# Splitting an expert table into f16 halves in earlier stages, and loading it as halves

## What is computed

```python
qh = (xb @ w_pq).reshape(t, PEER_HEADS, 2, PEER_QDIM // 2)
s = jnp.einsum('thpc,hpkc->thpk', qh, peer_keys)
s_top, i_top = lax.top_k(s, PEER_TOPK)
...                                   # 16 best of 256 pairs of each head: idx, softmax g
u = peer_u[idx]
a = jax.nn.gelu(jnp.einsum('td,ted->te', xb, u), approximate=False)
w = (g * a)
return jnp.einsum('te,ted->td', w, peer_v[idx])
```

## Time and profile before

| what | value |
|---|---|
| median of 3 runs | 4344.81 us (4338.82 to 4346.47) |
| profiled execution, its own time | 4337.67 us |
| its span | 4335.7 us |
| PE, DVE, ACT, POOL busy | 83%, 73%, 30%, 22% of the span |
| DMA | 856.46 MB, mean 198 GB/s |

### The profile page before, as it was taken

How to read it: one execution, slowest core, us unless ns; L and a number is a source line. 1 busy time by engine, 2 the same in 40 slices (tenths; PEclk the granted TensorE clock), 3 DMA queues, 4 the chain that set the end, 5 groups by cost and what they waited for, 6 DMA issues and landing times. The chain is left out here.

```text
span 4335.7 us, 59165 instructions
## 1 busy us (share of the span) xinstructions
PE 3612.2 (83%) x19538; PEld 1998.8 (46%) x19538; DVE 3183.3 (73%) x5656; ACT 1302.0 (30%) x2576; POOL 939.4 (22%) x1038
## 2 busy tenths in 40 slices
PE   6956468899689757487899999999999999999993
PEld 3535344455345423366345454544444454454442
DVE  1024431222459978899699999999899999999998
ACT  2131222211223233344233332333333333332331
POOL 0000000000000000000344444444443444444444
PEclk9966569999899878655899999999999999999996
DMA  2100020210211010266788888889888888888885
GB/s 92 63 26 1 0 84 29 99 38 0 84 61 38 22 62 0 79 194 193 293 337 328 340 330 327 331 323 341 314 329 326 326 334 324 341 325 319 334 329 184
DMA packets 238936, 856.46 MB, mean 198 GB/s; under 512 B 16080, under 2 KB 119312, under 8 KB 167440
## 3 DMA queue, kind: packets, MB, share of 16 engines
q0 software_dynamic: 73728, 536.90, 32.7%
q1 hardware_dynamic: 165136, 318.63, 21.2%
HBM read 792.55 MB, written 62.91 MB: 197 GB/s over the span
## 5 line engine op out<-in xcount | busy, mean ns | idle before, releaser
L1579 POOL COPY x_index<-expert 128x1 uint32 (+1 forms) x512 | 333.9, 652 | 2951.2 <-POOLq L1379 2068.0
L70 PE MATMUL x_ps_v<-x_v_hi,x_w_hi 128*128 128x512 f16 x1536 | 604.6, 394 | 134.4 <-DVE x_w_lo L1683 77.5
L1582 POOL DMA_INDIRECT x_rows<-in_peer_uv,x_index x512 | 581.9, 1137 | 406.9 <-POOL x_index L1579 393.1
L1653 DVE SCALAR_TENSOR_TENSOR acc<-x_rows,x_share,acc 128x1024 f32<-128x1024 f32 x512 | 654.8, 1279 | 0.0
L1737 PE MATMUL x_ps_a<-h_hi,x_u_hi 128*128 128x256 f16 (+1 forms) x2048 | 620.5, 327 | 18.4 <-ACT x_u_hi L1595 15.8
L1738 PE MATMUL x_ps_a<-h_lo,x_u_hi 128*128 128x256 f16 (+1 forms) x2048 | 620.2, 327 | 0.0
L71 PE MATMUL x_ps_v<-x_v_lo,x_w_hi 128*128 128x512 f16 x1536 | 603.8, 393 | 0.0
L72 PE MATMUL x_ps_v<-x_v_hi,x_w_lo 128*128 128x512 f16 x1536 | 602.3, 392 | 0.0
L1606 ACT ACTIVATE x_dots<-x_dots 128x1 f32<-128x1 f32 x512 | 103.9, 203 | 1328.4 <-DVE x_dots L1671 1328.4
L1671 DVE CUSTOM_DVE_ANT_0 x_rows<-h_lo,x_rows 128x1024 f32<-128x1024 f32 x256 | 312.4, 1220 | 124.5 <-DMA x_rows<-in_peer_uv,x_index 123.5
L1742 PE MATMUL x_ps_a<-h_hi,x_u_lo 128*128 128x256 f16 (+1 forms) x2048 | 374.6, 326 | 0.0
(11 more groups left out here) (286 smaller groups left out, 6398.2 us busy)
## 6 DMA issues: line engine op xcount, KB each, us to landing
x_u_st<-in_peer_u_t SPq DMA_DIRECT2D x128, 512.0 KB, 5.9
x_v_st<-in_peer_v SPq DMA_DIRECT2D x128, 512.0 KB, 5.8
gate_scratch<-g_out SPq DMA_DIRECT2D x24, 2048.0 KB, 8.7
x_gate<-gate_scratch SPq DMA_DIRECT2D x32, 1024.0 KB, 8.7
x_gate<-gate_scratch SPq DMA_DIRECT2D x32, 512.0 KB, 3.7
m_w_st<-in_w_merge SPq DMA_DIRECT2D x8, 1536.0 KB, 6.4
k_w_st<-in_w_route SPq DMA_DIRECT2D x16, 576.0 KB, 3.7
x_rows<-in_peer_uv,x_index POOLq DMA_INDIRECT x512, 6.9
```

Of the source, the lines that this page charges most:

```text
L70: pe.matmul(out, lhs_hi, rhs_hi, start=first, stop=False)
L1579: pool.tensor_copy(index[:, m % RING:m % RING + 1], R.expert[:, tile, bass.ds(hk, 1)]).then_inc(index_ok, 1)
L1582: pool.indirect_dma_start(rows[:, m % RING], None, uv_all, bass.IndirectOffsetOnAxis(ap=index[:, m % RING:m % RING + 1], axis=0)).then_inc ...
L1653: dve.scalar_tensor_tensor(R.acc[:, DT + tile], rows[:, r, D:2 * D], share[:, s:s + 1], R.acc[:, DT + tile], ALU.mult, ALU.add).then_inc(v ...
```

## The change

In project and merge a new helper, Ahead, reads all 128 tiles of table v (40 in project, 88 in merge) by DMAs that POOL issues, splits them with ACT (high half, times 4) and DVE (low half), and stores the two halves, 512 KB for a tile as before, in a scratch of device memory (v_scratch). It has two buffers: the load of tile n waits for the low half of tile n - 2, and stands behind its store. In project a split stands behind each of the ten evacuations of the values and behind each block of ten weight tiles; in merge, 4, 4 and 3 splits stand in the three blocks of a weight tile. Experts then loads the halves into one buffer for each of the four expert tiles, without splits; these loads wait for the last product of the group before. Each stage's semaphores are now cleared and given back when it ends, with one more barrier (release).

```diff
+class Ahead:
...
+    def load(self, pool, A, n, s, first=False):
+        if not first:
+            pool.wait_ge(self.v_lo_ok, n - 1)
+        pool.dma_start(self.st[:, s], A["peer_v"][n + self.first]).then_inc(self.v_in[s], 16)
+
+    def high(self, act, n, s, nth, first=False):
+        act.wait_ge(self.v_in[s], 16 * nth)
+        if not first:
+            act.wait_ge(self.v_out[s], 16 * nth - 16)
+        act.activation(self.out[:, s, 0], self.st[:, s], ACT.Copy, scale=VSCALE).then_inc(self.v_hi_ok, 1)
+
+    def low(self, dve, n, s):
+        dve.wait_ge(self.v_hi_ok, n + 1)
+        dve.scalar_tensor_tensor(self.out[:, s, 1], self.st[:, s], VSCALE, self.out[:, s, 0], ALU.mult,
+                                 ALU.subtract).then_inc(self.v_lo_ok, 1)
+
+    def store(self, pool, n, s):
+        pool.wait_ge(self.v_lo_ok, n + 1)
+        pool.dma_start(self.R.v_dram[n + self.first], self.out[:, s]).then_inc(self.v_out[s], 16)
+
+    def moves(self, pool, A, count):
+        self.load(pool, A, 0, 0, True)
+        self.load(pool, A, 1, 1, True)
+        with pool.Fori(0, count // 2 - 1) as i:
+            for s in range(2):
+                self.store(pool, 2 * i + s, s)
+                self.load(pool, A, 2 * i + (2 + s), s)
...
@@ project, ACT
                     act.activation(R.proj[:, m, t0:t0 + n_t], ps[:, slot, b, 0:n_t], ACT.Copy,
                                    scale=1 / WSCALE).then_inc(m_ev, 1)
+                    if turn is not None:
+                        ahead.high(act, TT + 6 * turn + (at + b), (at + b) % 2, 3 * turn + (TT // 2 + (at + b) // 2 + 1))
...
@@ merge
+        SHARE = (4, 4, 3)
...
@@ merge, ACT
+                    early, late = units(i, q, b)
+                    for v, slot, nth in early:
+                        ahead.high(act, v, slot, nth, isinstance(v, int) and v < 2)
                     wait_apart(act, mg_ok, n + 1)
                     act.activation(R.m_hi[:, m, t0:t0 + n_t], mg[:, s, 0:n_t], ACT.Copy).then_inc(mg_hi, 1)
+                    for v, slot, nth in late:
+                        ahead.high(act, v, slot, nth)
...
@@ Buffers
+    def release(self):
+
+        self.nc.clear_and_free_semaphores(self.stage)
+        self.stage = []
+        self.nc.all_engine_barrier()
...
@@ experts, SP
             def load_v(i, e, first=False):
-                n = E * i + e
-                if not first or e >= 2:
-                    sp.wait_ge(v_lo_ok, n - 1)
-                sp.dma_start(v_st[:, e % 2], v_all[n]).then_inc(v_in[e % 2], 16)
+                if not first:
+                    wait_apart(sp, v_mm, V_STEPS * i)
+                sp.dma_start(v[:, e], R.v_dram[E * i + e]).then_inc(v_in, 16)
...
@@ experts, ACT
-                        if b == 0:
-                            act.wait_ge(v_in[e % 2], 32 * i + 16 * (e // 2 + 1))
-                            if not first:
-                                act.wait_ge(v_mm, V_STEPS * i)
-                            act.activation(v_hi[:, e], v_st[:, e % 2], ACT.Copy, scale=VSCALE).then_inc(v_hi_ok, 1)
...
@@ experts, DVE
-                        if b == 0:
-                            dve.wait_ge(v_hi_ok, E * i + e + 1)
-                            dve.scalar_tensor_tensor(v_lo[:, e], v_st[:, e % 2], VSCALE, v_hi[:, e], ALU.mult,
-                                                     ALU.subtract).then_inc(v_lo_ok, 1)
...
@@ experts, PE
-                        pe.wait_ge(v_lo_ok, E * (i + 1))
+                        pe.wait_ge(v_in, 16 * E * i + 16 * E)
```

More of the change, by code:

```diff
@@ L65, with __init__ @@
 AB_ROW = 32
+V_EARLY = 40
+V_TILE = 11
+assert V_EARLY + KO * V_TILE == EXPERTS // P
+class Ahead:
+    def __init__(self, nc, c, R, name, first):
+        self.R, self.first = R, first
+        self.st = c.enter_context(nc.sbuf_tensor(name + "_v_st", [P, 2, D], f32))
+        self.out = c.enter_context(nc.sbuf_tensor(name + "_v_out", [P, 2, 2, D], f16))
+        sem = lambda n: R.semaphore(name + n)
+        self.v_in, self.v_out = [sem("_v_in0"), sem("_v_in1")], [sem("_v_out0"), sem("_v_out1")]
+        self.v_hi_ok, self.v_lo_ok = sem("_v_hi_ok"), sem("_v_lo_ok")
+    def load(self, pool, A, n, s, first=False):
[21 more added lines that the diff above has]
+                self.load(pool, A, 2 * i + (2 + s), s)
+        for s in range(2):
+            self.store(pool, count - 2 + s, s)
+            pool.wait_ge(self.v_out[s], 16 * (count // 2))
 def hi_lo(pe, out, lhs_hi, lhs_lo, rhs_hi, rhs_lo, first, last):
@@ L98, in project, with _ @@
         NV = 4
+        ahead = Ahead(nc, c, R, "p", 0)
         block = c.enter_context(nc.Block())
+        @block.gpsimd
+        def _(pool):
+            ahead.moves(pool, A, V_EARLY)
         @block.sync
@@ L199, in w_split @@
                                          ALU.mult, ALU.subtract).then_inc(w_lo_ok, 1)
-            m_items(dve, w_split)
+            w_split(dve, 0, 0, M_LOW, True)
+            for n in range(TT):
+                ahead.low(dve, n, n % 2)
+            w_split(dve, 1, 1, 0, False)
+            with dve.Fori(0, 5) as i:
+                for half in range(2):
+                    w_split(dve, 2 + half + 2 * i, half, 2 * i + 1, False)
+                    for b in range(3):
+                        ahead.low(dve, TT + 6 * i + (3 * half + b), (3 * half + b) % 2)
+            w_split(dve, 12, 0, 11, False)
         @block.tensor
@@ L227, with __init__, semaphore @@
 class Buffers:
-    pass
+    def __init__(self, nc):
+        self.nc, self.stack, self.stage = nc, ExitStack(), []
+    def semaphore(self, name):
+        self.stage.append(self.nc.alloc_semaphore(name=name))
+        return self.stage[-1]
+    def release(self):
+        self.nc.clear_and_free_semaphores(self.stage)
+        self.stage = []
+        self.nc.all_engine_barrier()
 def gated_attention(nc, A, R):
@@ L236, in gated_attention @@
         sb = lambda n, s, d: c.enter_context(nc.sbuf_tensor(n, s, d))
-        sem = lambda n: R.stack.enter_context(nc.semaphore(n))
+        sem = R.semaphore
         w_a2 = sb("a_w_a2", [2 * AB_ROW, HEADS * DK], f32)
@@ L674, in merge, with _, units @@
             "w_hi_ok w_lo_ok mm sig prod mg_ok mg_hi mg_lo".split()]
+        ahead = Ahead(nc, c, R, "m", V_EARLY)
+        SHARE = (4, 4, 3)
+        assert sum(SHARE) == V_TILE
         block = c.enter_context(nc.Block())
+        @block.gpsimd
+        def _(pool):
+            ahead.moves(pool, A, KO * V_TILE)
+        def units(i, q, b):
+            off = sum(SHARE[:b]) - q * V_TILE
+            each = [(2 * V_TILE * i + (off + r), (off + r) % 2, V_TILE * i + ((off + r) // 2 + 1)) for r in range(SHARE[b])]
+            return each[:2], each[2:]
         @block.sync
@@ L698, in _, with steps @@
         def _(act):
-            def steps(m, q):
+            def steps(m, q, i):
                 for b, (t0, n_t) in enumerate(BLOCKS):
@@ L739, in steps @@
                     dve.tensor_tensor(mg[:, s, 0:n_t], t1[:, 0:n_t], t2[:, 0:n_t], ALU.add).then_inc(mg_ok, 1)
+                    early, late = units(i, q, b)
+                    for v, slot, nth in early:
+                        ahead.low(dve, v, slot)
                     dve.wait_ge(mg_hi, n + 1)
@@ L742, in steps @@
                                       ALU.subtract).then_inc(mg_lo, 1)
+                    for v, slot, nth in late:
+                        ahead.low(dve, v, slot)
             split_lo(0, 0)
             split_lo(1, 1)
-            steps(0, 0)
+            steps(0, 0, 0)
             with dve.Fori(1, KO // 2) as i:
                 split_lo(2 * i, 0)
-                steps(2 * i - 1, 1)
+                steps(2 * i - 1, 1, i)
                 split_lo(2 * i + 1, 1)
-                steps(2 * i, 0)
-            steps(KO - 1, 1)
+                steps(2 * i, 0, i)
+            steps(KO - 1, 1, KO // 2)
         @block.tensor
@@ L1499, in experts @@
         NBD = len(DENSE)
-        u_st, v_st = sb("x_u_st", [P, 2, D], f32), sb("x_v_st", [P, 2, D], f32)
+        u_st = sb("x_u_st", [P, 2, D], f32)
         u_hi, u_lo = sb("x_u_hi", [P, E, KO, P], f16), sb("x_u_lo", [P, E, KO, P], f16)
-        v_hi, v_lo = sb("x_v_hi", [P, E, D], f16), sb("x_v_lo", [P, E, D], f16)
+        v = sb("x_v", [P, E, 2, D], f16)
         gate = sb("x_gate", [P, ND, E], f32)
@@ L1867, in build @@
             mix_norm(nc, A, R)
+            R.release()
             merged.close()
```

40 lines of the change are left out of this document (24 added, 16 removed).

## The result

The changed kernel takes 4464.59 us (median of 4 runs, 4459.1 to 4483.15), the kernel before 4341.83 beside it (4338.82 to 4346.47): ratio 1.0285, 95% interval 1.0263 to 1.0308. It is 2.9% slower. The forecast was 4318, so it missed the sign and the range.

The account below looks back on a forecast made before the run. The prediction took DVE, with PE behind it, to bound the expert stage. From 4337.67 us, -118 experts, +83 merge, +3 projection and +5 releases gave 4310.7, as a median 4318 us; range 4225 to 4400.

Parts of the forecast that it names:

- Experts, -118 forecast: Expert stage: removing four x_v_lo splits shortens a group from 69.1 to 65.4 us, over 32 groups -118 us.
- Nothing for this: Expert stage: v loads and the loads queued behind them come no later than before, v has 31 us to land; no cost.
- allowed for gathers: Expert stage: each gather lands 0.25 us later at the higher DMA share, three turns in a group, 0.8 us.
- Rival C: Expert stage: gathers landing 1 us later take most of the gain, leaving -48; median 4388 us, chance 0.12.
- the ring: Expert stage: four gather buffers turn in 11.2 us, passing three visits; the second half's ten visits take 37.3 us.
- Merge, +83 forecast: Merge: 44 turns of loading, splitting and storing v outlast the time PE gives, ending at 1175, +83 us.
- the turn of two buffers: Merge: store, load and two splits of one buffer form a chain of 8.7 us, against 6.8 us available.
- L: Merge: time from a POOL-issued v load's issue to its landing, taken as 4.9 us, between 3.5 and 6.9.
- rival B: Merge and projection: from 9.2 us a buffer turn the kernel is slower; at 10.5 the median is 4424 us; chance 0.15.
- rival A: Merge: POOL's loads land as fast as SP's, 3.5 us, so merge costs only 17 us; median 4252 us, chance 0.20.
- Projection, +3 forecast: Projection: buffer turns up to 8.65 us are hidden; the first two loads of 512 KB add 3 us.
- Releases, +5: Seven stages get a semaphore clear on POOL and one more barrier, 0.7 us each, +5 us.

Follow-up runs that it names:

- six rows alone: The changed kernel with six row buffers for the gathers in place of four and nothing else: 4307.67 us, ratio 0.9920 to the kernel before.
- spread loads: The changed kernel with each expert's v load also waiting for a hidden block of the new group: 4417.61 us; also combined with additional buffers ahead: 4302.21 us.
- the second kernel: A kernel with six row buffers for the gathers; with additional buffers ahead and v loads as in the changed kernel, it took 4190.2 us.
- more buffers: The changed kernel with four and four buffers in projection, three and three in merge, and some loops written out: 4344.97 us, ratio 1.0016.
- the experts alone: The changed kernel without splitting v ahead in projection and merge; v halves come from a table of random numbers: 4315.8 us, ratio 0.9949.

## Why the prediction was wrong

*What bounds the kernel before* was read rightly: DVE late, PE behind it, PE's own group at 62.3 us. The last is met, 62.8 us, where rows come in time (six rows alone). The group that was read, 69.1 us, is a little long: the mean is 68.5.

*Experts, -118 forecast, -32.7 measured: the largest error, 85 us.* The removed DVE work came out where and as large as stated, 4.1 us of a group's first part. The step that failed is the one on the v loads, "Nothing for this". It asked only whether v comes in time and found that it does. It did not ask what else is on the DMA engines when four loads that x_v_lo used to space are let go by one wait, with two of u behind them: the second part grew by 3.3 us a group, all of it before the last visit. Taking the burst apart brings that part from 46.7 to 44.1, and taking v's loads away from 46.9 to 44.2; spread loads give 1.2 us of it back in the first part (20.9 to 22.1). The rest, 0.8, is of the size that the prediction had allowed for gathers. With spread loads a group is 65.8 to 66.2 us. That this is near the forecast 65.4 is partly the long group that the forecast started from: against the mean of 68.5 it is a gain of 2.2 to 2.6 us, not 3.7.

Rival C named the gathers, with an end of -48 that was not far enough out and a chance of 0.12. But its mechanism, each of three turns landing 1 us later, is not what happened: one visit of sixteen waits 3.5 us longer. Its argument against, that v loads leave the gather-heavy second half, was wrong both ways. Before, two of the four stood in the first part; now all four stand at the end of the second by the marks of DVE and ACT, since PE is done with its v tiles 16 us before the next group's first Gelu (3177.94 and 3194.34 in the rows above).

Behind this lies a step that the prediction worked out but did not weigh: the ring. It put ten visits at 37.3 us by median landings and summed the halves to 61.7. In the trace the second part took 43.4 us already before, and 39.1 with six rows. A closed ring of four (the next gather starts only when a row is used up) has no reserve when one of its rows is late, and the median of landings doesn't show that. The removed split is worth 33 us with four rows and the burst; with six rows 156 us of DVE's work are worth 137. The forecast of -118 described the second kernel, not the one at hand.

*Merge, +83 forecast, +131.9 measured, 49 us off.* The mechanism is the one named, the turn of two buffers, and three buffers show it. The term that was mis-sized is the turn, 9.54 us from the first split to the 87th, not 8.7; times 43 that is 36 us. The trace takes it apart (means of the turns in merge):

| piece of a turn | forecast | measured |
|---|---|---|
| POOL, from the low half to the load's issue | 1.17 | 1.39 |
| the load, issue to landing | 4.9 | 5.45 |
| the two splits | 2.47 | 2.28 |
| ACT and DVE late for a split | 0.2 | 0.42 |

The largest part is L, the landing of the load: 4.9 had been chosen between 3.5 and 6.9 without a row for it, and the mean is 5.45. (The forecast's ends of 7.15 and 10.5 leave out the 0.2 that its middle has.) The other 13 us: the first split is 3.6 us later in the stage than the forecast had it, the last splits take 6.3 us, not 3.4, and the end of the stage 9.9 us from the last low half (1236.10 to 1245.99), not 3.8. By rival B's own point, 9.2 us a turn, the change was bound to lose; B stood at 0.15.

Under rival B the prediction held that issues are not delayed by DVE's work, from the median gather issue of 1.04 us. For plain loads the changed kernel bears that out. For gathers the median hides that some issues are longer beside DVE's work; the last section has the numbers. Merge's issues are plain, so the forecast lost nothing by this.

The Trainium skill, "DMA: Bandwidth & Descriptors", section "Anatomy of one DMA", leads to an estimate of 3.2 us for such a load by its figures. The shortest here is 4.1 and the median 5.2, so the trace does not agree for loads that go beside stores of the same queue, and rival A, which leaned the same way, fell.

*Projection, +3 forecast, +17.8 measured.* It was to be hidden up to a turn of 8.65. With more buffers it is +4.5: about the 3 us of the first loads, and the other 13 us went with more buffers, the turn again (9.8 us in the median there).

*Releases, +5.* With the releases alone ahead of the experts, projection and merge are +0.3 and +2.1. In attention the kernels differ by more than that without a difference in its code (359.1 us with spread loads, 367.8 with the experts alone), so the small terms can't be read there.

The three errors, 85, 49 and 15, sum to 149 of the 150 us between the forecast for one execution, 4310.7, and the profiled 4460.8.

## What to carry to other kernels

Before work is taken off the engine that is late, look at what else was paced by it: the loads that waited for each removed instruction now start together. Then ask which wait stands where they start. The share of the DMA engines there (1.02 against 0.89 in the mean) is a sign, and no more; the place of the wait within a round, visit by visit, showed the harm at once.

Where the late engine itself waits for a closed ring of transfers, give the ring one or two more buffers first; here only then was a saved microsecond of that engine worth nearly one.

A stream of load, split and store needs as many buffers as the time given to one tile goes into its whole chain: 9.5 us over 3.4 (the 6.8 us a turn that PE gives, for two tiles) are nearly three here. A chain summed from medians comes out short (8.9 here, where the mean turn is 9.5).

## What the runs showed of the hardware

- A stage that ends with stores of GpSimd's queue took 9.3 to 9.5 us from the last store's issue to the next stage's first load, though in the changed kernel the DMA engines had nothing to move in the last 5 of them; with SyncE's queue it took 3.6.

```profile
1236.00:1238.00 2.00, 0.00 (x0) 0.00 (x0) 0.10 (x1) 0.00 (x0) 0.54 (x1) 0.50 0.11 45
1238.00:1240.00 2.00, 0.00 (x0) 0.00 (x0) 0.00 (x0) 0.00 (x0) 0.00 (x0) 0.50 0.54 217
1240.00:1241.00 1.00, 0.00 (x0) 0.00 (x0) 0.00 (x0) 0.00 (x0) 0.00 (x0) 0.50 0.00 0
...
1244.00:1246.00 2.00, 0.00 (x0) 0.00 (x0) 0.00 (x0) 0.00 (x0) 0.00 (x0) 0.50 0.00 0
```

- GpSimd issued each of merge's 88 plain loads in 527 to 537 ns. 18 of these issues overlapped a split on DVE that reads two tiles of SBUF, and stayed in the same range. Issues of gathers differ: in the changed kernel's experts they took 957 to 1012 ns where DVE had nothing to do (35 issues), and 1213 to 1955 ns beside x_u_lo (26 issues) and 1479 ns in the median where it was a visit's acc that overlapped them longest (106 issues). Beside dot products with h_lo the median was 962 ns (99 issues), so it is not all of DVE's work; no run separates what does it.
- Six gathers in flight are not faster ones: they land in 7.7 us in the median (six rows alone) against 7.8 for four with the same loads, and with spread loads in 8.8 against 7.5. They still deliver sooner where it counts: DVE's waits fall from 226.4 to 87.9 and from 167.6 to 99.7 us.
- GpSimd stood 3.4 to 3.5 us before every 110th gather, in the kernel before and in the changed one, for nothing that the profile shows.
- TensorE's granted clock in merge was 0.88 in the changed kernel and 1.00 in the same kind of stretch before, a mean between its levels of 2.4 and 1.2 GHz (1.00 and 0.50). It fell where PE waited for m_mg: below, PE stands from 884 to 892 us, and in the 4 us after it goes on it does 10 matmuls, against 20 in as long a time at 1.00. So PE lost clock as well as waiting, and its busy time rose from 312.64 to 341.15 us for the same 1728 matmuls.

```profile
884.00:888.00 4.00, 0.00 (x0) 0.00 (x0) 1.23 (x1) 1.30 (x2) 0.00 (x0) 0.93 0.43 174
888.00:892.00 4.00, 0.00 (x0) 0.00 (x0) 3.12 (x4) 1.97 (x3) 2.13 (x4) 0.50 0.63 184
892.00:896.00 4.00, 3.93 (x10) 1.45 (x11) 0.56 (x2) 1.06 (x1) 0.00 (x0) 0.50 0.90 335
...
904.00:908.00 4.00, 4.00 (x20) 1.77 (x19) 1.99 (x2) 2.42 (x4) 1.06 (x2) 1.00 0.32 129
```

- In the experts the granted clock was 0.98 with four rows and 1.00 with six (six rows alone), and PE's busy time of a group fell from 63.8 to 62.5 us: part of what the six rows gain is this.
